# The memory's norm factor moved from the memory products to the keys and values, with the first loads in another order

## The reference

```python
def _rms_norm(x, g):
    y = xf * lax.rsqrt(jnp.mean(xf * xf, axis=-1, keepdims=True) + EPS)
    return (y * g.astype(jnp.float32)).astype(x.dtype)
...
def _memory_cross_attention(h, mem_n, w_xq, w_xkv, w_xo):
    q = (h @ w_xq).reshape(B, S, XATT_HEADS, XATT_HEAD_DIM)
    kv = mem_n @ w_xkv
    k, v = jnp.split(kv, 2, axis=-1)
    ...
    s = jnp.einsum('bshd,bmhd->bhsm', q, k) * (XATT_HEAD_DIM ** -0.5)
    p = jax.nn.softmax(s, axis=-1)
    o = jnp.einsum('bhsm,bmhd->bshd', p, v).reshape(B, S, D_MODEL)
    return o @ w_xo
...
for l in range(DEPTH):
    h = _rms_norm(x, norm_mix_pre[l])
    ...
    mem_n = _rms_norm(mem, norm_mem[l])
```

## Time and profile before

| | us |
|---|---|
| median of 3 runs | 1119.89 (1118.78 to 1120.2) |
| the profiled execution, its own time | 1118.98 |
| its span in the trace | 1117.2 |
| TensorE busy | 1103.5 (99%) |
| ScalarE busy | 565.2 (51%) |
| VectorE busy | 563.9 (50%) |
| GpSimd busy | 672.3 (60%) |
| share of TensorE in the chain that ended last | 95% |

### The profile page before, as it was taken

How to read it: one execution, slowest core, us unless ns; L and a number is a source line. 1 busy time by engine, 2 the same in 40 slices (tenths; PEclk the granted TensorE clock), 3 DMA queues, 4 the chain that set the end, 5 groups by cost and what they waited for, 6 DMA issues and landing times.

```text
span 1117.2 us, 20125 instructions
## 1 busy us (share of the span) xinstructions
PE 1103.5 (99%) x8258; PEld 1026.6 (92%) x8258; DVE 563.9 (50%) x1049; ACT 565.2 (51%) x895; POOL 672.3 (60%) x352
## 2 busy tenths in 40 slices
PE   8999999999999999999999999999999999999997
PEld 7999999998898999899999999999978969999996
DVE  6688558455515641234567865593644344212333
ACT  7645854434645544444464567544346545444443
POOL 4866767627673457654477658675378444576442
PEclk9999999999999999999999999999999999999999
DMA  7543444624543655545544434445255254555553
GB/s 286 179 143 133 160 133 161 180 89 151 198 161 124 205 182 187 188 173 187 189 170 170 151 133 152 139 164 157 72 188 190 96 187 152 188 188 181 182 185 114
DMA packets 63339, 183.40 MB, mean 164 GB/s; under 512 B 18576, under 2 KB 19088, under 8 KB 63248
## 3 DMA queue, kind: packets, MB, share of 16 engines
q1 hardware_dynamic: 47936, 172.48, 44.1%
q10 hardware_dynamic: 15312, 9.64, 3.3%
HBM read 179.47 MB, written 2.62 MB: 163 GB/s over the span
## 4 chain that ended last, share of the span: by engine, by line
PE 95%; DMA 2%; ACT 1%; DVE 1%; issue 1%; POOL 0%; SPq 0%; ACTq 0%; DVEq 0%; POOLq 0%
PE psum L484 27%; PE psum L485 27%; PE psum L486 26%; DMA sb_raw<-weights 2%; PE psum L632 1%; PE psum L959 1%; PE psum L938 1%; PE psum L676 1%; PE psum L659 1%; PE psum L562 1%; PE psum L853 1%; PE psum L846 1%; PE psum L643 1%; PE psum L728 1%; ACT sb_high L373 0%
## 5 line engine op out<-in xcount | busy, mean ns | idle before, releaser
L383 POOL TENSOR_TENSOR sb_low<-sb_raw,sb_high 128x1024 fp32r<-128x1024 f32 x258 | 620.8, 2418 | 350.7 <-ACT sb_high L373 336.0
L373 ACT ACTIVATE sb_high<-sb_raw 128x1024 fp32r<-128x1024 f32 x322 | 340.4, 1061 | 430.0 <-DMA sb_raw<-weights 378.7
L484 PE MATMUL psum<-sb_h_high,sb_high 128*128 128x256 f32 x1664 | 471.6, 283 | 0.7 <-DVE sb_low L383 0.7
L486 PE MATMUL psum<-sb_h_high,sb_low 128*128 128x256 f32 x1664 | 469.6, 282 | 0.0
L485 PE MATMUL psum<-sb_h_low,sb_high 128*128 128x256 f32 x1664 | 469.5, 282 | 0.0
L484 PEld LDWEIGHTS psum<-sb_h_high,sb_high 128*128 128x128 f32 x1664 | 314.6, 189 | 3.0 <-issue 1.1
L485 PEld LDWEIGHTS psum<-sb_h_low,sb_high 128*128 128x128 f32 x1664 | 313.0, 188 | 0.9
L486 PEld LDWEIGHTS psum<-sb_h_high,sb_low 128*128 128x128 f32 x1664 | 312.7, 188 | 0.0
L383 DVE TENSOR_TENSOR sb_low<-sb_raw,sb_high 128x1024 fp32r<-128x1024 f32 x64 | 101.7, 1596 | 38.3 <-ACT sb_high L373 37.8
L2046 DVE SCALAR_TENSOR_TENSOR sb_sq<-sb_th,psum 128x512 f32<-128x512 f32 x22 | 15.1, 688 | 148.4 <-ACT sb_th L1462 148.4
L1806 DVE SCALAR_TENSOR_TENSOR sb_conv<-psum,sb_param,sb_conv 128x255 f32<-128x255 f32 (+1 forms) x144 | 58.3, 474 | 46.7 <-ACT sb_conv L1262 46.7
(11 more groups left out here) (280 smaller groups left out, 1529.5 us busy)
## 6 DMA issues: line engine op xcount, KB each, us to landing
sb_raw<-weights SPq DMA_DIRECT2D x322, 512.0 KB, 3.2
sb_pre_gain<-pre_gains ACTq DMA_DIRECT2D x6, 512.0 KB, 4.4
sb_post_gain<-post_gains ACTq DMA_DIRECT2D x6, 512.0 KB, 4.2
sb_kx<-mem SPq DMA_DIRECT2D x2, 512.0 KB, 4.3
sb_x<-x SPq DMA_DIRECT2D x1, 1024.0 KB, 10.8
t_dram<-sb_sq ACTq DMA_DIRECT2D x4, 256.0 KB, 2.9
out<-sb_x SPq DMA_DIRECT2D x4, 256.0 KB, 2.1
m_dram<-sb_m ACTq DMA_DIRECT2D x8, 64.0 KB, 2.0
```

The source lines that it names most:

```text
L373: nc.scalar.activation(high[:, n % HIGHS, :], raw[:, n % RAWS, :], ACT.Copy).then_inc(high_ready, 1)
L383: eng.tensor_tensor(low[:, k, :], raw[:, k, :], high[:, n % HIGHS, :].bitcast(F32), ALU.subtract).then_inc(low_ready[k], 1)
L484: pe.matmul(out, a[0], b[0], start=start, stop=False, **kw)
L486: return pe.matmul(out, a[1], b[0], start=False, stop=stop, **kw)
```

## The change

It takes the norm's factor out of the memory's way to the products and puts it in later.

- The memory is loaded to another place (`attn_t`) and is turned and multiplied as it is, times the gain alone. VectorE's multiply of the tiles goes, and TensorE's turns wait for the load alone.
- SP loads n = 0 ahead of the memory, the positions and n = 3 ahead of x.
- ScalarE copies one piece (not two) ahead of `mem_high`, and all up to n = 3 right behind it; the load of the pre-norm gain is issued behind `mem_high`. VectorE makes the low parts of n = 1 and 3 (not 2 and 3), both ahead of the memsets that pass x on; GpSimd makes that of n = 2.
- For n = 1 to 3 TensorE does the matmuls on the high weights first and waits for the low part only then (`high_first`).
- TensorE does 11 warm-up matmuls, not 16.
- The squares of the memory stand in layer 0 on ScalarE behind the index logits' relus, the roots on GpSimd behind the low part of n = 16. SP writes the 256 factors to DRAM behind weights n = 28 and reads them back behind n = 32 as a row on every partition (`mem_row`).
- The values are multiplied in their copy on ScalarE, by `scale`. The keys done by then are multiplied by GpSimd in one instruction in the delta rule's stage, the later ones by VectorE when it takes them out of PSUM, in place of ScalarE's copy. TensorE waits for the former ahead of the cross scores.

```diff
-WARM_START = 16
+WARM_START = 11
...
-            return n in (0, 2, 3) or (part, i, b) in (("xv", 2, 0), ("xv", 2, 1), ("xv", 3, 0), ("xo", 3, 1), ("nk", 0, 1))
+            return n in (0, 1, 3) or (part, i, b) in (("xv", 2, 0), ("xv", 2, 1), ("xv", 3, 0), ("xo", 3, 1), ("nk", 0, 1))
...
-            for c in range(TILES):
-                sp.dma_start(mem_block(kx_t)[:, c, :], mem_in[c * P:(c + 1) * P]).then_inc(mem_loaded[c], 16)
             for n in range(RAWS):
                 sp.dma_start(raw[:, n, :], weights[n]).then_inc(raw_loaded[n], 16)
+                if n == 0:
+                    for c in range(TILES):
+                        sp.dma_start(mem_block(attn_t)[:, c, :], mem_in[c * P:(c + 1) * P]).then_inc(mem_loaded[c], 16)
                 if n == 2:
+                    sp.dma_start(y_t[:, 0:S].bitcast(I32), pos_in.broadcast_to([P, S])).then_inc(pos_loaded, 16)
+                if n == 3:
                     sp.dma_start(x, x_in.rearrange("(c p) d -> p c d", p=P)).then_inc(x_loaded, 16)
-                    sp.dma_start(y_t[:, 0:S].bitcast(I32), pos_in.broadcast_to([P, S])).then_inc(pos_loaded, 16)
...
+                if n == HALF_AT[0, "bq", 0, 0]:
+                    sp.wait_ge(mem_pool, 2 * TILES)
+                    for c in range(TILES):
+                        sp.dma_start(bass.AP(m_dram.tensor, c * P, [[1, P], [1, 1]]), mem_rs[:, c:c + 1]).then_inc(row_stored, 16)
+                if n == HALF_AT[0, "bq", 2, 0]:
+                    sp.wait_ge(row_stored, 16 * TILES)
+                    sp.dma_start(mem_row, bass.AP(m_dram.tensor, 0, [[0, P], [1, S]])).then_inc(row_loaded, 16)
...
-                pe.wait_ge(mem_dve, c + 1)
+                pe.wait_ge(mem_loaded[c], 16)
...
+                def high_first(o, n, act):
+                    pe.wait_ge(high_ready, n + 1)
+                    w = high[:, n % HIGHS, :], low[:, n % RAWS, :]
+                    for k in range(KT):
+                        pe.matmul(o, w[0][:, k * P:(k + 1) * P], act[0][:, k, :], start=(k == 0), stop=False)
+                        pe.matmul(o, w[0][:, k * P:(k + 1) * P], act[1][:, k, :], start=False, stop=False)
+                    weights_here(n)
+                    for k in range(KT):
+                        mm = pe.matmul(o, w[1][:, k * P:(k + 1) * P], act[0][:, k, :], start=False, stop=(k == KT - 1))
                     return mm
...
+                pe.wait_ge(*keys_scaled.at(layer, "xk"))
...
-            highs(act, done, 2)
+            highs(act, done, 1)
             act.wait_ge(param_loaded, 16)
...
-            highs(act, done, HIGHS - 1)
-
-            act.wait_ge(mem_pool, 2 * TILES)
-            act.wait_ge(mem_act, TILES)
+            act.dma_start(pre_gain_t[:, :], pre_gains[0:1, :].broadcast_to([P, D])).then_inc(pre_loaded, 16)
+            highs(act, done, HIGHS)
...
+                if layer == 0:
+                    for c in range(TILES):
+                        act.wait_ge(mem_loaded[c], 16)
+                        nc.scalar.activation(sq_t[:, :], mem_block(attn_t)[:, c, :], ACT.Square, scale=D ** -0.5, accum_out=mem_ss[:, c:c + 1])\
+                            .then_inc(mem_squared, 1)
+                        act.wait_ge(mem_squared, c + 1)
...
                 pool.wait_ge(*dve_norm.at(layer, ("xn", "mix", 1, 1)))
+                if layer == 0:
+                    low_parts(ahead(("logits", 1, 1), 2))
+                    for c in range(TILES):
+                        pool.wait_ge(mem_squared, c + 1)
+                        nc.gpsimd.tensor_tensor(mem_rs[:, c:c + 1], mem_ss[:, c:c + 1], eps_col, ALU.add).then_inc(mem_pool, 1)
+                        pool.wait_ge(mem_pool, 2 * c + 1)
+                        nc.gpsimd.tensor_tensor(mem_rs[:, c:c + 1], mem_rs[:, c:c + 1], neghalf[:, 0:1], ALU.pow).then_inc(mem_pool, 1)
                 low_parts(ahead(("squares", 3), 2))
...
+                nc.gpsimd.tensor_tensor(kx[:, 0:keys_done, :], kx[:, 0:keys_done, :], heads(mem_row, keys_done), ALU.mult)\
+                    .then_inc(keys_scaled.sem, keys_scaled.mark("xk"))
...
             mem_lows(1, 0, mem_turned)
+            low_parts(4)
             dve.wait_ge(x_loaded, 16)
...
-            low_parts(3)
...
+                dve.wait_ge(*slots.at(layer, ("xk", 3)))
+                V.tensor_tensor(kx[:, 6:8, :], bank(("xk", 3)).rearrange("p (b t) -> p b t", b=2), heads(mem_row, 2), ALU.mult)\
+                    .then_inc(dve_gdn.sem, dve_gdn.mark(("xk", 3)))
```

More of the change, by code:

```diff
@@ L190, in program @@
         tiny_t = sb("tiny", 480)
+        mem_row_t = sb("mem_row", S)
         gain_t = sb("post_gain", D, F32, rc_t)
@@ L566, in _ @@
                 for i in range(2 if layer == 0 else 0):
-                    wide(("xk", i), mem_gain, (act_copy, ("xk", i)), range(4), {} if i else {k: (mem_low_ready, KT * layer + k + 1) for k in range(KT)})
+                    o = claim(("xk", i), (act_copy, ("xk", i)), range(4))
+                    for b in range(2):
+                        at, n = o[:, b * S:(b + 1) * S], HALF_AT[layer, "xk", i, b]
+                        if i == 0 and b == 0:
+                            mm = wide_half(at, n, mem_gain, {k: (mem_low_ready, k + 1) for k in range(KT)})
+                        else:
+                            mm = high_first(at, n, mem_gain)
+                        mm.then_inc(slots.sem, mark(slots, ("xk", i) if b else (("xk", i), "first")))
                 if layer > 0:
@@ L1193, in _ @@
                 if layer == 0:
-                    highs(act, done, HIGHS)
                     for j in range(4):
```

45 lines of the change are left out of this document (21 added, 24 removed).

## The result

The changed kernel takes 1125.58 us in the median of 6 runs (1124.18 to 1129.0), the kernel before 1119.57 (6 runs on the same chip). The ratio is 1.0056, with a 95% interval of 1.0046 to 1.0066: 6.0 us slower. The forecast was 1122.0 with a range to 1123.4. The direction was right, the size was not, and the time lies outside the range.

A forecast was written before the change was run, and what follows sets the result against it. TensorE was taken to bound the kernel, busy 1103.5 of 1117.2 us. +0.8 at n=5 and +1.35 at n=17 gave +2.15 us on the median of 1119.89: 1122.0 us, range 1120.3 to 1123.4 (8 in 10).

The forecast's parts named there:

- The rest: Remaining parts, among them keys' multiplies, row stores and row load on SP's queue, and matmul order: together nothing added.
- +0.8 at n=5: Opening: the first product on x starts 0.8 us later than before, though n=0 starts 1.8 us earlier.
- +1.35 at n=17: Index stage: TensorE newly waits 1.35 us for GpSimd's low part, delayed by the roots of the memory; bounds 1.0 to 1.9.
- First product at 9.35: Opening: TensorE's first weight product, n=0, starts at 9.35 us instead of 11.12.
- Low n=3 held up by GpSimd: Opening: VectorE's low n=3 waits for GpSimd's low n=2 and ends at 16.6 us instead of 14.9.
- The split at 16.55 decides, not the load: Opening: x lands by 15.4 us, so VectorE's low n=3, not x's load, sets when the squares of x start.
- 24.77 + 2.4 - 0.95 - 0.35: Opening: sum for the start of ScalarE's h_high, 25.9 us, from its old start, the delay and two recovered waits.
- (a): Rival, opening: low n=3 isn't held up, leaving -0.65 + 1.35 = +0.7 us, 1120.6; chance 0.17.
- (c): Rival: neither low n=3 held up nor a wait at n=17, -0.65 us, 1119.2; chance 0.05.
- (b): Rival, index stage: no wait at n=17, the sums being ready sooner; +0.8 us alone, 1120.7; chance 0.11.
- (d): Rival, opening: GpSimd's low n=2 gets in ahead of VectorE's low n=1; +3.1 us in all, 1123.0; chance 0.07.
- (e): Rival, opening: with fewer warm-up matmuls TensorE's clock rises late; +4.9 us if at 20 us, 1124.8; chance 0.04.

The follow-up runs named there:

- f1: Changed kernel without the row stores and row load; the row is made on chip by two TensorE transposes and a ScalarE copy: 1121.88 us, ratio 1.0028.
- e1: Changed kernel without the two row stores, the row being read from a gain instead: 1121.63 us, ratio 1.0022.
- e2: Kernel before plus only two stores of 128 four-byte numbers behind weights n=28, the row load and ScalarE's wait for it: 1123.92 us, ratio 1.0044.
- e3: Changed kernel with the two row stores issued from ScalarE's queue at about 81 us instead of SP's: 1124.58 us, ratio 1.005.
- e4: Changed kernel with GpSimd's two roots of the memory behind the low part of n=17 instead of n=16: 1124.56 us, ratio 1.005.
- f3: f1 with VectorE instead of GpSimd making the low part of n=2: ratio 1.0031.
- f2: f1 with the load of the positions behind x instead of ahead of n=3: ratio 1.0028.
- f4: f1 with positions behind x, low n=2 on VectorE and GpSimd's roots behind the low part of n=17: ratio 1.0002.

## Why the prediction was wrong, point by point

**The step that failed** is in "The rest": the row stores "delay a weight load by a microsecond at worst, where low is done several us ahead of its use: nothing". Two things were wrong in it. The size: the weights behind took 10.1, 9.8 and 8.1 us instead of some 3.2, so they were late by 5 to 7 us, not one. I had priced the stores by their bytes and their place in the queue, and no row of the kernel before has a store of that shape, so an upper bound was needed that I didn't give. And the cover: I looked at how far the low part is ahead of TensorE, but the first victim was ScalarE, whose wait for raw data stands in one written order with the convolution copies. TensorE lost 3.5 us through ScalarE, VectorE and a PSUM bank, not through a low part, and 1.5 more through the clock. By the ratios the term is 3.1 us (changed kernel against f1) to 3.8 (against e1), with intervals of some 1 us each, by the spans 4.7 and 4.4, and 4.9 alone (e2).

**The terms of the sum** were near. The forecast had +0.8 at n=5 and +1.35 at n=17; the trace has +1.49 and +0.99, and without the stores the kernel measured 2.5 (e1) to 3.1 us (f1) over before, where 2.15 was forecast.
- First product at 9.35: it came at 10.00 in the profiled run and at 9.49 to 9.80 in e1, e3, e4, f1 and f3. The first loads land some tenths later or earlier from run to run.
- Low n=3 held up by GpSimd: right. It took 2.63 instead of 1.22 and ended 1.09 after GpSimd's, as in the earlier trace rows (1.08).
- "The split at 16.55 decides, not the load": wrong by 0.7. x landed at 17.2, 12.8 us after its issue, not by 15.4. With the positions behind n=2, the loads moved only 139 and 229 GB/s in the two halves of the microsecond from 10.0, where 400 is usual; with the positions behind x (f2) that hole isn't there, x landed at 15.2, near the forecast's 15.4, and the memset came at 16.66 and n=5 at 28.56: the forecast's 16.7 and 28.5. The step left out the positions' load, which the change put ahead of x and which goes in 1 KB pieces.
- The wait at n=17: right in kind, 0.99 instead of 1.35; e4 takes it away.
- Keys' multiply on GpSimd, 2.91 and 3.46 us, and on VectorE, 0.68: as forecast (3.0, 3.6, 0.69), and nobody waits for them.
- Two slips in the sums changed little. In "24.77 + 2.4 - 0.95 - 0.35" only 0.26 of the last term has a row behind it. And (a) and (c) are priced with n=5 0.65 earlier, although by their own bound for x (15.4) the same sum gives 0.45; f4, where neither limit holds, measured 0.14.
- Rivals: (a) and (c) fell with low n=3, (b) with the wait at n=17. (d) did not come: VectorE's low n=1 was over at 13.74, GpSimd began at 13.59. (e) did not come where it was put: from n=0 on the matmuls are 0.12 us apart at a granted clock of 1.00, with 11 warm-up matmuls as with 16. The clock's price came elsewhere, behind the wait at 111 us, where no rival had it.
